# A gated feed-forward layer in split fp32: the up projection by Strassen's seven block products, the down projection as a stage of its own

## The reference

```python
def conv_ffn(x, prefix, g_ffn, w_up, conv_w, conv_b, w_down):
    h = rmsnorm(x, g_ffn)
    up = h @ w_up                                   # 1088 x 1024 @ 1024 x 5632
    ext = jnp.concatenate([prefix, up], axis=1)     # two rows of state ahead of each sequence
    c = depthwise_causal_conv(ext, conv_w, width=3) + conv_b
    gate, val = jnp.split(c, 2, axis=-1)
    return (jax.nn.silu(gate) * val) @ w_down, ext[:, -2:]
```

## Time and profile before

| | |
|---|---|
| time, median of 3 runs | 1458.73 us (1458.33 to 1461.59) |
| profiled execution | 1458.96 us, its span 1457.2 us |
| PE busy | 98% of the span, 8708 matmul records |
| DVE, ACT, POOL busy | 53%, 26%, 3% |
| PE's mean granted clock | 0.990 |
| DMA | 93.35 MB, mean 64 GB/s |

### The profile page before, as it was taken

How to read it: one execution, slowest core, us unless ns; L and a number is a source line. 1 busy time by engine, 2 the same in 40 slices (tenths; PEclk the granted TensorE clock), 3 DMA queues, 4 the chain that set the end, 5 groups by cost and what they waited for, 6 DMA issues and landing times.

```text
span 1457.2 us, 21729 instructions
## 1 busy us (share of the span) xinstructions
PE 1421.2 (98%) x8708; PEld 1380.2 (95%) x8708; DVE 776.6 (53%) x928; ACT 378.7 (26%) x701; POOL 41.8 (3%) x91
## 2 busy tenths in 40 slices
PE   5999999999999999999999999999999999999995
PEld 4999989899899999999999999999999999999995
DVE  6123544444455542376565646474747474747476
ACT  5112225445361122152121202020202020202025
POOL 1000100000000011110000000000000000000000
PEclk9999999999999999999999999999999999999998
DMA  9111101222235423211111010101111111102003
GB/s 260 49 42 37 49 31 60 77 72 75 74 106 167 135 90 90 74 59 44 59 29 59 29 59 29 59 29 59 32 55 39 49 47 41 56 32 64 10 16 123
DMA packets 117844, 93.35 MB, mean 64 GB/s; under 512 B 12024, under 2 KB 108224, under 8 KB 117767
## 3 DMA queue, kind: packets, MB, share of 16 engines
q1 hardware_dynamic: 117807, 92.83, 20.3%
HBM read 78.65 MB, written 15.26 MB: 64 GB/s over the span
## 4 chain that ended last, share of the span: by engine, by line
PE 95%; DVE 2%; ACT 1%; DMA 1%; SPq 0%; issue 0%; DVEq 0%; ACTq 0%
PE PS L594 70%; PE PS L937 16%; PE PS L734 1%; PE PS L757 1%; PE PS L613 1%; PE PS L744 1%; PE PS L947 1%; DMA xtok<-in_x_prompt_dram 1%; ACT ysq_junk L1315 1%; PE PS L708 1%; PE PS L1008 0%; PE PS L871 0%; DVE xtok L1370 0%; PE PS L916 0%; DVE h_lo L1347 0%; ACT ytok L1051 0%
## 5 line engine op out<-in xcount | busy, mean ns | idle before, releaser
L594 PE MATMUL PS<-h_hi,up_hi 128*128 128x364 f32 (+2 forms) x1656 | 375.5, 335 | 0.0
L594 PE MATMUL PS<-h_lo,up_hi 128*128 128x364 f32 (+2 forms) x1656 | 366.8, 330 | 0.0
L594 PE MATMUL PS<-h_hi,up_lo 128*128 128x364 f32 (+2 forms) x1656 | 365.5, 329 | 0.0
L594 PEld LDWEIGHTS PS<-h_hi,up_hi 128*128 128x128 f32 x1656 | 282.8, 189 | 14.2 <-issue 10.0
L594 PEld LDWEIGHTS PS<-h_hi,up_lo 128*128 128x128 f32 x1656 | 287.6, 189 | 1.7 <-issue 1.7
L594 PEld LDWEIGHTS PS<-h_lo,up_hi 128*128 128x128 f32 x1656 | 288.0, 189 | 0.0
L1340 DVE TENSOR_TENSOR up_lo<-raw,up_hi 128x1024 fp32r<-128x1024 f32 x86 | 115.4, 1342 | 104.8 <-ACT up_hi L1051 104.8
L1720 DVE TENSOR_TENSOR y<-PS,y 128x1092 f32<-128x1092 f32 x80 | 103.7, 1296 | 89.6 <-PE PS L937 89.6
L1647 DVE TENSOR_TENSOR ext_val<-PS,rms_row 128x728 f32<-128x728 f32 x21 | 19.3, 917 | 168.8 <-PE PS L594 168.8
L937 PE MATMUL PS<-act_hi,dn_hi 128*128 128x364 f32 (+1 forms) x480 | 105.6, 328 | 0.0
L937 PE MATMUL PS<-act_lo,dn_hi 128*128 128x364 f32 (+1 forms) x480 | 105.6, 328 | 0.0
(11 more groups left out here) (253 smaller groups left out, 1584.8 us busy)
## 6 DMA issues: line engine op xcount, KB each, us to landing
raw<-in_w_up_dram SPq DMA_DIRECT2D x44, 512.0 KB
raw<-in_w_in_dram SPq DMA_DIRECT2D x22, 512.0 KB
raw_dn<-in_w_down_dram SPq DMA_DIRECT2D x11, 1024.0 KB, 5.9
gates_scratch<-gate_st SPq DMA_DIRECT2D x16, 546.0 KB, 2.7
gates<-gates_scratch SPq DMA_DIRECT2D x16, 546.0 KB, 4.6
xtok<-in_x_prompt_dram SPq DMA_DIRECT2D x8, 512.0 KB, 8.6
xcol<-in_x_prompt_dram SPq DMA_DIRECT2D x8, 512.0 KB, 3.5
raw<-in_w_out_dram SPq DMA_DIRECT2D x8, 512.0 KB
```

The source lines that it names most:

```text
L594: ins = pe.matmul(PS[:, 3 * s + piece, 0:width], w[:, first_k + n, :], x[:, k, first:first + width], start=(n == 0 and q == 0), stop=(n == ...
```

## The change

The up projection is done by Strassen's scheme. The 1024 rows of h are halved (`KH` = 4 tiles each), the output is halved into gate and value (one tile j of each), and the tokens are cut into quarters of 272 (`HALF`), two quarters to a half h. For each j and h, a round q = 2j + h, seven products p1 to p7 of 4 k x 3 terms = 12 matmuls of 272 columns replace eight; sums and differences of weight blocks (s1 to s4) and of token blocks (t1 to t4) are their operands, and additions recombine the results. The token blocks are made once after the project stage. The weight blocks, seven slots a tile of 128 x 512 (a11, a12, a22 straight from the weights), are made for each j: ACT copies the high part, DVE the sums and the low part. Results leave PSUM in six pieces of 272 columns by DVE additions (c11, c12, c22 for each q) and four copies by ACT a round (p1, v, r, c21). They land unscaled in `ext`, and DVE then scales the row of 1088 in SBUF (`scale_rows`). The first tap goes from DVE to ACT (`first_tap`), and the small copies of states and samples go from ACT to POOL.

The product of gate and value is stored to DRAM (`act_scratch`) instead of being split at once, and so is y (`y_scratch`). When all 22 tiles are done, the down projection runs by three token segments. Segment 0 (384) takes 22 row steps with all eight PSUM banks, and a row of w_down and one of act are loaded for each. Segments 1 and 2 (384 and 320) run in 32 units of 33 matmuls with column blocks of w_down, 704 KB each. The 44 transposes of line 916 become seven at the end. There is no hardware loop in the feed-forward part.

In the project stage the sum x + product goes through one buffer `xT`, from which SP stores it. The diff, cut to what orders the work (`product` on PE is 12 matmuls, `pe.wait_ge(lo_done[x], ...)` ahead of them for even q, and `full[x]` behind them):

```diff
     SP, project stage:
                 if m < 4:
                     c = CHUNK_OUT + m + 4
                     load_chunk(c, c % 2, out_views(m + 4, m % 2))
-                else:
-                    load_chunk(c, c % 2, up_views((m - 4) // 2, m % 2))
...
+                sp.wait_ge(acc_free, FILL_OUT - FILL_BRANCH + m + 1)
+                sp.dma_start(y_dram[m], xT[:, 0:T]).then_inc(y_spilled, 16)
     ACT, project stage:
+                if m:
+                    act.wait_ge(y_spilled, 16 * m)
+                copy(xT[:, 0:SEQ - P], aux[:, 0:SEQ - P]).then_inc(aux_free, 1)
     PE:
+            def p4(q):
+                pe.wait_ge(r_copied, q + 1)
+                product("a22", q, q % 2, False)
...
+            for q in range(2, NHALF):
+                p6(q)
+                p4(q - 1)
+                p5(q)
+                p3(q - 1)
+                if q + 1 < NHALF:
+                    p1(q + 1)
+                p7(q)
+                p2(q)
     ACT:
+            def take_r(q):
+                act.wait_ge(full["s3"], q + 1)
...
+                copy(r_copy[:, :], PS[:, q % 2, 0:HALF]).then_inc(r_copied, 1)
...
+            def first_tap(j, val):
+                u = 2 * j + val
+                act.wait_ge(spread, u + 1)
...
+                act.activation(dst[:, :], ext[:, 2 * (j % 2) + val, 2:2 + NCONV], ACT.Identity, bias=cw[:, 3, ch:ch + 1],
+                               scale=cw[:, 2, ch:ch + 1]).then_inc(tap_done, 1)
...
+            for j in range(1, NFF):
+                split_slot("a12", j)
+                take_v(2 * j)
+                take_c21(2 * j - 1)
+                split_slot("s3", j)
+                split_slot("a22", j)
+                first_tap(j - 1, 0)
+                split_slot("s4", j)
+                take_p1(2 * j + 1)
+                first_tap(j - 1, 1)
+                silu(j - 1)
+                take_r(2 * j)
+                take_v(2 * j + 1)
...
+                take_c21(2 * j)
...
     DVE:
+            for j in range(1, NFF):
+                weight_sum_3(j)
+                add_c22(2 * j - 1)
+                add_c11(2 * j - 1)
+                split_slot_lo("a12", j)
+                split_slot_lo("s3", j)
+                scale_rows(j - 1, 0)
+                split_slot_lo("a22", j)
+                add_c12(2 * j - 1)
+                scale_rows(j - 1, 1)
+                more_taps(j - 1, 0)
+                split_slot_lo("s4", j)
...
+                more_taps(j - 1, 1)
...
+                product(j - 1)
     POOL:
+            def spread_samples(j, val):
+                pool.wait_ge(scaled, 2 * j + val + 1)
+                row, ch = ext[:, 2 * (j % 2) + val, :], val * NFF + j
+                samp = row[:, EXT_S:EXT].rearrange("p (b t) -> p b t", b=DEC_B)
+                pool.tensor_copy(tpack[:, 0:CSTATE, ch], row[:, EXT_S - CSTATE:EXT_S])
+                pool.tensor_copy(tpack[:, CSTATE:NROW, ch].rearrange("p (b w) -> p b w", b=DEC_B),
+                                 samp[:, :, DEC_T - CSTATE:DEC_T])
+                pool.tensor_copy(spaced(row)[:, :, CSTATE:], samp).then_inc(spread, 1)
```

More of the change, by code:

```diff
@@ L574, in _ @@
+            for j in range(6, NTILE):
+                store_y(j)
             sp.wait_ge(dram_copy, 16 * 3)
@@ new lines, in product @@
+            def product(x, q, bank, start):
+                f_hi, f_lo = factors[x]
+                if q % 2 == 0:
+                    pe.wait_ge(lo_done[x], q // 2 + 1)
+                for k in range(KH):
+                    for t, (w, f) in enumerate(((s_hi[x], f_hi), (s_hi[x], f_lo), (s_lo[x], f_hi))):
+                        ins = pe.matmul(PS[:, bank, 0:HALF], w[:, k, :], f(q % 2, k), start=start and k == 0 and t == 0,
+                                        stop=k == KH - 1 and t == 2, skip_group_check=not start)
+                ins.then_inc(full[x], 1)
@@ L1173, in _, with split_slot @@
             act.wait_ge(pads_done, 1)
-            def project(m, half, last=False, between={}):
+            def split_slot(x, j):
+                if x in ("a11", "a12"):
+                    act.wait_ge(val_in, 16 * j + 16)
+                    k0 = 0 if x == "a11" else KH
+                    src = raw[:, 0, k0:k0 + KH]
+                elif x == "a22":
+                    act.wait_ge(gate_raw_in, 16 * j + 16)
+                    src = raw[:, 1, KH:KD]
+                else:
+                    act.wait_ge(sums_done, sum_count(x, j))
+                    src = {"s1": s1_raw, "s2": s2_raw, "s3": s3_raw, "s4": s4_raw}[x][:, :, :]
+                if j:
+                    act.wait_ge(full[x], 2 * j)
+                copy(s_hi[x][:, :, :], src).then_inc(slot_hi, 1)
@@ L1190, in project @@
-                if not last:
-                    split_hi(half, (m - half) + (CHUNK_OUT + 2))
-            with act.Fori(0, 3) as i:
-                for half in range(2):
-                    project(i * 2 + half, half)
-            project(KD - 2, 0)
-            def ffn_input(k):
-                act.wait_ge(acc_free, FILL_OUT - FILL_BRANCH + k + 1)
-                if k < KD - 1:
-                    act.wait_ge(mx_read, k + 1)
-                act.activation(h2_hi[:, k, :], y[:, k, :], ACT.Copy, scale=gffn[:, k:k + 1]).then_inc(h2_hi_done, 1)
@@ L1318, in _ @@
[L1318 to L1329 removed]
+            take_c21(0)
@@ new lines, in y_squares @@
+            def y_squares(p, part):
+                first, end = ((0, 4 * P), (4 * P, 6 * P), (6 * P, D))[part]
+                act.wait_ge(turn_free, 4 * p + part + 3)
+                for n in range(3):
+                    rows = TILE_ROWS[3 * p + n]
+                    act.activation(sq_junk2[0:rows, 0:end - first], ytok[p][0:rows, n, first:end], ACT.Square,
+                                   accum_out=ssq2[0:rows, part, 3 * p + n:3 * p + n + 1]).then_inc(ysq_done, 1)
+                    act.wait_ge(ysq_done, 9 * p + 3 * part + n + 1)
@@ L1924, in _ @@
             pool.wait_ge(pads_done, 1)
[L1926 to L1928 removed]
+            for m in range(KD):
                 pool.wait_ge(sq_done, m + 1)
[L1930 to L1938 removed]
```

1346 lines of the change are left out of this document (856 added, 490 removed).

## The result

The changed kernel takes 1500.47 us (median of 4 runs, 1498.92 to 1502.17) against 1458.67 before: a ratio of 1.028, 95% interval 1.026 to 1.030. It is slower by 42 us, where 88 were predicted. The profiled execution took 1501.96, its span 1500.1, with a mean granted clock of 0.958 (0.990 before).

The account below looks back on a forecast made before the run. TensorE, busy 98%, was taken as the bound. From 1458.96, matmuls -57, transposes -4, one-off waits +8, +13, +3, +8 gave 1430; loop waits +64, clock +46 and +7.5 gave 1547 us, range 1448 to 1573.

Parts of the forecast that it names:

- they take turns: one POOL copy for one DVE instruction: Rounds: three POOL copies pass behind three DVE instructions, 3.9 us after the value row; PE waits 3.05 in 21 periods, +64.
- The rest of the loop: Rounds: after those copies come first tap 1.21, silu 1.13 and take_r 0.39, making 6.6 us from the scaled value row.
- The clock term: Rounds: PE's clock falls to the low level behind its waits, costing 2.2 us a period, +46 (0 to 63).
- Matmuls: Up projection: 3696 matmuls of 272 columns at 0.127 us, 469.4 us instead of 526.5, a gain of 57.
- rival 3: Up projection: 272 columns cost as much as 320 because the weight load binds; about 1566 us, chance 0.04.
- (a): Project stage: xT must be stored before the next x is copied in, the store issued behind a weight load; +8 us.
- (d): Falls of the clock behind the waits that come once, five at 1.5 us: +7.5.
- (b): Between last project gemm and steady rounds: DVE has 26.7 us of work beside 23.8 of PE; +13 (5 to 20).
- (c): End of the rounds +3 us (0 to 6); first column units, their loads landing and being split, +8 (3 to 14).
- Rival 1: Rounds: POOL slips through or its short copies do not block, so the loop waits 0.5 us; 1448 us, chance 0.23.
- Rival 2: Rounds: POOL's copies are blocked but PE's clock stays full; 1501 us, chance 0.11.

Follow-up runs that it names:

- experiment 1: Changed kernel with POOL making the copy into ext, which ACT's first tap waits for, ahead of the two into tpack: 1455.24 us.
- experiment 2: Changed kernel with the three small sample and tpack copies of each row moved from POOL to ACT, into first_tap: 1452.81 us.
- experiment 8: Changed kernel with ACT copying p7's result (take_r) before the value row's first tap and the silu instead of behind them: 1440.38 us.
- experiment 3: Changed kernel with fourteen matmuls whose result nobody reads put ahead of p4(2j), to fill PE's wait: 1489.43 us.
- Experiment 7: Changed kernel with POOL's 16-element copy of the value row made as eight copies of 2: 1553.43 us.
- experiment 4: Changed kernel with SP issuing the store of xT ahead of the next weight load, for the first four m of the project stage: 1483.25 us.

## Why the prediction was right or wrong

- **The direction and the mechanism** were right: PE's columns fall as computed, and more than that is lost in waits in the rounds, on POOL's copies behind DVE's taps (experiments 1, 2 and 8), with falls of the clock behind them (experiment 3). The size was not: +42 instead of +88.
- **The step that failed** is "they take turns: one POOL copy for one DVE instruction". From the one place of the mixer, a copy of 512 elements, it was carried to copies of 2 and 16. These take 0.2 us, and one passes in the gap between the taps (the 801.20 row), so three copies wait for two instructions, not three. The rule of the Trainium skill ("SBUF — State Buffer", section "Who interferes with whom") agrees with the trace here too, a copy that missed the gap waited 1.35 us for a tap; that every copy would miss it was read into one row. The copies took 2.9 after the scaled row instead of 3.9; the wait is 1.9 with its edge, not 3.05, **40 instead of 64**. The rest of the loop held: from the scaled row to p4(2j) it took 5.6 (799.85 to 805.41) instead of 6.6, nearly all of the difference in the copies.
- **The clock term** (2.2 a period, +46) hung on that step: 0.9 a period, some **18**. Experiment 7 made the wait that was predicted, and the clock then took 2.1. So both errors have one root. That its time, 1553 us, lies near the predicted 1547 is in part luck: it holds the 19 of the project stage, where the sum had 8.
- **Matmuls**: 0.1255 instead of 0.127, 463.9 us, 5 better; the spacing stayed on the slope of the longer ones, and rival 3 falls.
- **One-off waits**: (a) was mis-sized, 11.0 of waits instead of 8, and with the clock's 0.93 in that stage +19.3. (d) was too small: five falls at 1.5 were for all places, but the project stage alone lost 8, and the start of the rounds ran at a granted 0.82 from 651 to 700 us. (b) 6.0 + 3.8 at the start and a longer r_copy wait, beside the 13; its working does not come out, as 13 products of 1.524 and the 2.1 of the 18 small matmuls make 21.9, not 23.8. (c) units 5.8 for wm_lo beside 8.
- **Rival 1** (1448, unblocked): its loop, worked out from single rows, was good to 0.1 us (0.42 and 0.45 in the row in experiments 2 and 1), and those two kernels took 1453 and 1455. Rival 2, the clock that stays, is what experiment 3 shows: waits without falls cost 11 to 15 less.
- The range to 1573 held the time; the forecast's own range, 1514 to 1575, did not, and its ends do not follow from the sum (with the +7.5 they are 1522 and 1568). The time is nearer to rival 2's 1501, but for another reason: the wait was shorter, and the clock did fall, behind 12 of 21 waits. Why one wait is followed by a fall and the next is not, no run settles.

## What to carry to other kernels

A chain of waits is only as true as the order of instructions in it: ask of each copy on the path whether it needs what stands ahead of it on its engine, or only stands there. Here one such move (experiment 8) made the whole conflict of POOL and DVE harmless, and two changes of order (experiments 1 and 4) were worth 45 and 17 us. And a price read at one size of an instruction (a lock, a wait) is a price for that size: look for the smallest like it before carrying it to small ones.

## What the runs showed of the hardware

- A POOL copy of 2 to 16 elements gets through in the gap between two dependent DVE instructions (the taps) with both inputs in SBUF, one in each gap besides the copy that had waited; a copy that has missed the gap waits for the whole next instruction, 1.3 us for a copy that takes 0.2 alone.
- Of 20 waits of PE of 1.8 us in the row, 23 to 25 us apart, 11 were followed by a fall of the granted clock, and so was the one of 3.2 ahead of them; of 20 waits of 3.1 (experiment 7) 19 were, and the one of 4.5 ahead of them; of the 40 waits of 0.4 (experiments 1 and 2) none was. A period with a fall was 1.5 us longer.
- ACT's first tap, 1104 columns with a scale and a bias column, took 1.31 us, where 1092 columns with a scale alone, written as fp32r, took 1.20.
